# Opening both blocks of a two-block network on unscaled pairs, with the norms computed behind the first chunks

## The reference

```python
def first_block(x, ...):                      # DEPTH = 2
    cos, sin = rope_tables(positions, A_HEAD_DIM)
    for l in range(DEPTH):
        h = rms_norm(x, norm_mix[l])          # x * rsqrt(mean(x*x) + eps) * gain
        (m_qk, m_v, m_o, m_i, m_f, r_x, r_g, a_q, a_k, a_v, a_qi, a_ki, a_w, gates) = jnp.split(
            h @ w_in[l], split_at, axis=-1)
        ...  # y_a: mLSTM of m_*; y_b: gelu(r_g) * gated LRU of a causal conv of r_x;
        ...  # y_c: attention over the 64 keys that an indexer (a_qi, a_ki, a_w) selects; q, k, qi, ki get rope
        x = x + (g_a * (y_a @ w_b[0]) + g_b * (y_b @ w_b[1]) + g_c * (y_c @ w_b[2])) @ w_out[l]
        h = rms_norm(x, norm_ffn[l])
        ff_g, ff_u = jnp.split(h @ ffn_up[l], 2, axis=-1)
        x = x + (jax.nn.gelu(causal_dwconv(ff_g, ...)) * ff_u) @ ffn_down[l]
    return rms_norm(x, norm_final)
# second block: h = rmsnorm(x, gain) with 16 meta tokens ahead; h @ w_in gives z, x, B, C, dt, b, c, h;
# y1 = group_rmsnorm(ssd(x, B, C, dt) * silu(z)); y2 = group_rmsnorm(c * conv(b * h));
# x = x + [y1, y2] @ w_out; then a mixture of 16 experts (top 2) and a last norm.
```

## Time and profile before

| | |
|---|---|
| time, median of 3 runs | 1719.89 us (1718.14 to 1720.11) |
| time of the profiled execution | 1718.21 us |
| its span | 1716.3 us |
| PE busy | 1616.0 us (94%), 11632 matmuls |
| DVE busy | 1300.1 us (76%) |
| ACT busy | 951.9 us (55%) |
| POOL busy | 43.2 us (3%) |

### The profile page before, as it was taken

One profiled execution on the slowest core, in us unless ns is written; L12 is line 12 of the kernel. 1 busy time (PEld: TensorE's weight loads), 2 busy tenths in 40 slices (PEclk: granted clock), 3 DMA queues, 4 the chain that ended last, 5 costly groups with the idle time before them and its releaser, 6 DMA issues.

```text
span 1716.3 us, 28017 instructions
## 1 busy us (share of the span) xinstructions
PE 1616.0 (94%) x11632; PEld 1508.1 (88%) x11632; DVE 1300.1 (76%) x1567; ACT 951.9 (55%) x990; POOL 43.2 (3%) x43
## 2 busy tenths in 40 slices
PE   3998999999997988999999997799999999999998
PEld 3898999999997988999999997698899788888886
DVE  6699676676666699677676667885895788898886
ACT  5647454554444646555454444554553677777774
POOL 0100001000000010001000000000000000000000
PEclk9999999999998999999999999899999899999999
DMA  7444535555555444535555555254445499999993
GB/s 204 148 123 131 165 123 172 166 190 182 180 183 143 147 124 134 162 123 172 171 187 187 178 184 158 74 172 123 123 148 190 168 358 352 362 352 369 353 353 130
DMA packets 222399, 328.92 MB, mean 192 GB/s; under 512 B 20832, under 2 KB 179168, under 8 KB 222304
## 3 DMA queue, kind: packets, MB, share of 16 engines
q1 hardware_dynamic: 222304, 327.56, 57.8%
HBM read 326.49 MB, written 1.05 MB: 191 GB/s over the span
## 4 chain that ended last, share of the span: by engine, by line
PE 77%; DVE 15%; issue 3%; ACT 3%; DMA 1%; POOL 0%; SPq 0%; DVEq 0%; ACTq 0%
PE bank L2021 23%; PE bank L2022 23%; PE bank L2023 23%; DVE w_lo L1197 2%; ACT w_hi L697 1%; DVE work L1249 1%; DVE work L1354 1%; PE bank L2375 1%; DMA w_raw<-in_w_in 1%; DVE w_lo L1650 1%; PE bank L2481 1%; DVE work L1679 1%; DVE work L1302 1%; DVE work L1372 1%; PE bank L2534 1%
## 5 line engine op out<-in xcount | busy, mean ns | idle before, releaser
L1197 DVE TENSOR_TENSOR w_lo<-w_raw,w_hi 128x2048 fp32r<-128x2048 f32 x158 | 362.7, 2296 | 138.9 <-ACT w_hi L697 138.2
L2021 PE MATMUL bank<-act_h,w_hi 128*128 128x256 f32 (+1 forms) x1408 | 408.7, 290 | 27.9 <-DVE act_l L1233 9.5
L2023 PE MATMUL bank<-act_h,w_lo 128*128 128x256 f32 (+1 forms) x1408 | 399.8, 284 | 0.0
L2022 PE MATMUL bank<-act_l,w_hi 128*128 128x256 f32 (+1 forms) x1408 | 399.7, 284 | 0.0
L697 ACT CAST w_hi<-w_raw 128x2048 fp32r<-128x2048 f32 x158 | 300.5, 1902 | 43.0 <-PE bank L2023 34.3
L2021 PEld LDWEIGHTS bank<-act_h,w_hi 128*128 128x128 f32 x1408 | 269.6, 191 | 36.8 <-issue 31.8
L2022 PEld LDWEIGHTS bank<-act_l,w_hi 128*128 128x128 f32 x1408 | 269.8, 192 | 0.6
L2023 PEld LDWEIGHTS bank<-act_h,w_lo 128*128 128x128 f32 x1408 | 269.2, 191 | 0.0
L2022 PE MATMUL bank<-u_l,w_hi 128*128 128x256 f32 x768 | 217.3, 283 | 0.0
L2023 PE MATMUL bank<-u_h,w_lo 128*128 128x256 f32 x768 | 216.9, 282 | 0.0
L2021 PE MATMUL bank<-u_h,w_hi 128*128 128x256 f32 x768 | 215.9, 281 | 0.0
(11 more groups left out here) (446 smaller groups left out, 2911.8 us busy)
## 6 DMA issues: line engine op xcount, KB each, us to landing
w_raw<-in_w_in SPq DMA_DIRECT2D x88, 1024.0 KB, 5.5
w_raw<-in_ffn_up SPq DMA_DIRECT2D x48, 1024.0 KB, 5.2
w_raw<-in_e_gate SPq DMA_DIRECT2D x26, 1024.0 KB, 7.1
w_raw<-in_ffn_down SPq DMA_DIRECT2D x24, 1024.0 KB, 5.0
w_raw<-in_e_up SPq DMA_DIRECT2D x23, 1024.0 KB, 7.1
w_raw<-in_e_down SPq DMA_DIRECT2D x23, 1024.0 KB, 7.3
w_raw<-in_w_out SPq DMA_DIRECT2D x16, 1024.0 KB, 5.2
w_raw<-in_w_branch SPq DMA_DIRECT2D x12, 1024.0 KB, 5.1
```

The costliest lines, as they stand in the source:

```text
L1197: V.tensor_tensor(w_lo[c % RING][:], w_raw[c % RING][:], w_hi[c % RING][:].bitcast(F32), ALU.subtract).then_inc(sem[f"lo_ready{c % RING}"], 1)
L2021: mm(out, a_hi, b_hi, start=first, stop=False, skip_group_check=True)
L2022: mm(out, a_hi, b_lo, start=False, stop=False, skip_group_check=True)
L2023: return mm(out, a_lo, b_hi, start=False, stop=last, skip_group_check=True)
```

## The change

**First block.** All chunks c below `SCALED_FROM` (10) multiply the pair of x*gain. The pair is written while the residual sums of the layer before still come. The norm's sum runs on PE behind chunk 0, and `before` holds no scaled tiles any more. Chunks 0..3 (`RAW_OUT`) are read out of PSUM by DVE, multiplied by `u_r`, into `raw_out`, from where ACT and DVE go on as before; for 4..9 the rope tables are multiplied by `u_r` instead, and the small projections get a multiply of their own. From c=10 on the scaled pair is used as before; it is made in `side` of c=4..9. `small_lower` and `decay_base` move from ahead of chunk 0 to c=1 and c=2, ACT's sin and cos of the tables into c=1 of the first layer. The last FFN round is written out with `ffn_hidden` ahead of the split of the next layer's chunk 0 (it was behind it).

**Second block.** z0 and z1 come first and multiply the unscaled pair (`RAW_2`). Both norms come from one pass over the squares: PE sums them by token with and without the squared gain (`both_sums`), DVE and ACT work on columns of 128 x 2 (`both_norms`), PE turns them to rows (`rows_of_tokens`, between the halves of chunk 1). The meta tokens are normalised in the FFN before. The residual `hx` is written at c=2..5 (`stream_2`). Everything that hung on x, B, C and the SSD stands two chunks later; `SC_STEPS` is unchanged.

The numbers of the order:

```diff
+SCALED_FROM = 10
+RAW_OUT = 4
...
+RAW_2 = 2
+SECTION_2 = ([("z", i) for i in range(RAW_2)] + [("x", i) for i in range(4)] + [("B", i) for i in range(2)]
+             + [("C", i) for i in range(2)] + [("z", i) for i in range(RAW_2, 4)] + [("c", i) for i in range(4)] + [("h", i) for i in range(4)]
...
-SSD_STEPS = (14, 16, 18, 20)
+SSD_STEPS = (16, 18, 20, 22)
```

SP, ahead of the first layer (only the column of inverse frequencies is loaded first, the rest of the constants, 448 KB, last; `par` ahead of the second chunk):

```diff
+            sp.dma_start(cst[:, K_INV:K_INV + 1], consts[:, K_INV:K_INV + 1], allow_slow_non_contiguous=True)\
+                .then_inc(sem["freq_loaded"], 16)
             load(0, 0, source(0, 0))
             sp.dma_start(x_t[:], xT.rearrange("(k p) t -> p k t", p=P)).then_inc(sem["x_loaded"], 16)
+            sp.dma_start(par_all[:], par_1.rearrange("l p n -> p l n")).then_inc(sem["par_loaded"], 16)
             load(0, 1, source(0, 1))
-            sp.dma_start(par_all[:], par_1.rearrange("l p n -> p l n")).then_inc(sem["par_loaded"], 16)
+            sp.dma_start(cst[:, 0:K_INV], consts[:, 0:K_INV]).then_inc(sem["const_loaded"], 16)
```

ACT (`before`, `side`, the end of the FFN):

```diff
             def before(L):
-                norm(L)
                 split(L, 2)
-                need(act, "small_landed", L, 64)
-                nc.scalar.copy(small_h, small_raw).then_inc(sem["small_hi"], 1)
-                need(act, "lam_abs", L, 1)
-                A(lt[1], lt[0], ACT.Exp, scale=-1.0).then_inc(sem["lam_exp"], 1)
+                raw_deviation(L, 0)
 
...
+                if 5 <= c <= 8:
+                    i = c - 5
+                    need(act, "scaled", L, 2 * i + 2)
+                    nc.scalar.copy(act_h[:, 2 * i:2 * i + 2, :], norm_f[i % 2]).then_inc(sem["act_hi"], 1)
...
+                ffn_gate(L, N_FF - 1)
+                split(L, MIX + 2, N_FF - 1)
+                ffn_mid(L, N_FF - 1)
+                ffn_hidden(L, N_FF - 1)
+                split(L, MIX + 3, N_FF - 1)
+                split(L, MIX + 4, N_FF - 1)
+                if L < DEPTH - 1:
+                    for i in range(4):
+                        raw_upper(L + 1, 0, i)
+                        raw_square(i)
```

DVE, first block:

```diff
+            def of_tokens(count):
+                return u_r.unsqueeze(1).to_broadcast([P, count, T])
+
+            def scaled_pair(L, i):
+
+                if i >= 2:
+                    need(dve, "act_lo", L, i - 1)
+                for h in range(2):
+                    k = 2 * i + h
+                    STT(norm_f[i % 2][:, h, :], x_t[:, k, :], pm[L][:, M_NORM + k:M_NORM + k + 1], u_r,
+                        ALU.mult, ALU.mult).then_inc(sem["scaled"], 1)
+
+            def scaled_lower(L, i):
+                need(dve, "act_hi", L, i + 1)
+                V.tensor_tensor(act_l[:, 2 * i:2 * i + 2, :], norm_f[i % 2],
+                                act_h[:, 2 * i:2 * i + 2, :].bitcast(F32), ALU.subtract).then_inc(sem["act_lo"], 1)
...
                 g = GROUP0[c]
+                ps = main[g % 2][:].rearrange("p (b t) -> p b t", b=2)
+                if c < RAW_OUT:
+                    need(dve, "group_done", L, g + 1)
+                    V.tensor_tensor(raw_out[c % 2], ps, of_tokens(2), ALU.mult).then_inc(sem["raw_out"], 1)
+                    ps = raw_out[c % 2]
...
             def before(L):
-                norm(L)
+                add_squares(L, 0, u_sq)
                 split(L, 2)
+                need(dve, "std_ready", L, 1)
+                step(V.reciprocal(u_r, u_std))
+
+            def small_lower(L):
                 need(dve, "small_hi", L, 1)
                 V.tensor_tensor(small_l, small_raw, small_h.bitcast(F32), ALU.subtract).then_inc(sem["small_lo"], 1)
...
+                if c == 1:
+                    small_lower(L)
+                if c == 2:
+                    decay_base(L)
...
+                    own(V.tensor_tensor(sin_r, sin_t[:], u_r, ALU.mult))
+                    own.settle()
+                    V.tensor_tensor(cos_r, cos_t[:], u_r, ALU.mult).then_inc(sem["rope_tables"], 1)
+                    need(dve, "small_done", L, 1)
+                    V.tensor_tensor(small_s, psum[6][:, 0:T], u_r, ALU.mult).then_inc(sem["small_scaled"], 1)
...
+                if 6 <= c <= 9:
+                    scaled_lower(L, c - 6)
+                if 4 <= c <= 7:
+                    scaled_pair(L, c - 4)
...
+                ffn_conv(L, N_FF - 1)
+                split(L, MIX + 2, N_FF - 1)
+                ffn_product(L, N_FF - 1)
+                ffn_hidden(L, N_FF - 1)
+                split(L, MIX + 3, N_FF - 1)
+                split(L, MIX + 4, N_FF - 1)
...
+                    if i and L < DEPTH - 1:
+                        raw_lower(L + 1, 0, i - 1)
+                    elif i:
+                        raw_lower_2(i - 1)
+                if L < DEPTH - 1:
+                    raw_lower(L + 1, 0, 3)
+                else:
+                    raw_lower_2(3)
```

DVE, second block (`both_norms` follows the split of chunk 2, `scaled_2` the read-out of z0):

```diff
+            def both_norms():
+
+                dve.wait_ge(sem["stat_act"], STAT_STD)
+                step(V.reciprocal(r_1, std_1))
+                step(V.tensor_tensor(var_2, psum[6][:, 1:4:2], r_1, ALU.mult))
+                V.tensor_tensor(var_2, var_2, r_1, ALU.mult).then_inc(sem["stat_dve"], 1)
+                dve.wait_ge(sem["stat_act"], STAT_STD_2)
+                step(V.reciprocal(std_2, std_2))
+                V.tensor_tensor(r_12, r_1, std_2, ALU.mult).then_inc(sem["stat_dve"], 1)
+
+            def scaled_2(i):
+
+                for k in (2 * i, 2 * i + 1):
+                    STT(norm_f2[:, k, META:TM], x_t[:, k, :], gain_u[:, k:k + 1], rows_r[:, 1, :], ALU.mult, ALU.mult)\
+                        .then_inc(sem["scaled"], 1)
+
+            def scaled_lower_2(i):
+                need(dve, "act_hi", DEPTH, i + 1)
+                V.tensor_tensor(act2_l[:, 2 * i:2 * i + 2, :], norm_f2[:, 2 * i:2 * i + 2, :],
+                                act2_h[:, 2 * i:2 * i + 2, :].bitcast(F32), ALU.subtract).then_inc(sem["act_lo"], 1)
+
+            def stream_2(i):
+
+                for k in (2 * i, 2 * i + 1):
+                    STT(hx[:, k, META:TM], x_t[:, k, :], p2[:, Q_NFIN + k:Q_NFIN + k + 1], rows_r[:, 0, :],
+                        ALU.mult, ALU.mult).then_inc(sem["scaled"], 1)
+
...
+                if c < RAW_2:
+                    for half in range(2):
+                        g = 2 * c + half
+                        need(dve, "group_done", DEPTH, g + 1)
+                        V.tensor_tensor(zs[:, g, :], psum[g % 4][:, 0:T], rows_r[:, 1, :], ALU.mult)\
+                            .then_inc(sem["z_raw"], 1)
...
+                if 2 <= c <= 5:
+                    stream_2(c - 2)
```

PE (the bank wait, the operands of a chunk, the opening of a layer, the sums and the opening of the second block):

```diff
+                if c < RAW_OUT:
+                    need(pe, "raw_out", L, c + 1)
...
+                x_h, x_l = (u_h, u_l) if c < SCALED_FROM else (act_h, act_l)
+                if c == SCALED_FROM:
+                    need(pe, "act_lo", L, 4)
...
-                norm(L, 0)
                 for c in range(MIX):
                     chunk(L, c)
+                    if c == 0:
+                        norm(L, 0)
                     side(L, c)
...
+            def both_sums():
+
+                need(pe, "squares", DEPTH, 4)
+                for k in range(KT):
+                    for s in range(2):
+                        ins = mm(psum[6][:, 2 * s:2 * s + 2], norm_f2[:, k, META + s * P:META + s * P + P],
+                                 gain_2[:, k, :], start=k == 0 and s == 0, stop=k == KT - 1, skip_group_check=True)
+                ins.then_inc(sem["stat_pe"], 1)
+
+            def rows_of_tokens():
+
+                pe.wait_ge(sem["stat_dve"], STAT_R)
+                for n, r in enumerate((r_1, r_12)):
+                    for s in range(2):
+                        ins = mm(psum[7][:, n * T + s * P:n * T + s * P + P], r[:, s:s + 1].to_broadcast([P, P]), ident,
+                                 start=n == 0 and s == 0, stop=True, skip_group_check=True)
+                ins.then_inc(sem["stat_pe"], 1)
...
+            chunk_2(0)
+            both_sums()
+            chunk_2(1, rows_of_tokens)
+            for c in range(2, MIX_2 - 1):
```

More of the change, by code:

```diff
@@ L945, in layer @@
                 own_each = 1
[L946 removed]
+                with act.Fori(1, N_FF - 1) as n:
                     own.enter(n - 1, own_each)
@@ L964, in _ @@
             act.wait_ge(sem["par_loaded"], 16)
+            for i in range(4):
+                raw_upper(0, 0, i)
+            split(0, 1)
+            for i in range(4):
+                raw_square(i)
             for L in range(DEPTH):
@@ L2078, in chunk @@
                 ins.then_inc(sem["group_done"], 1)
-            rows_first = [(m, k) for m in range(2) for k in range(KT)]
-            pairs_first = [(m, 2 * i + j) for i in range(4) for m in range(2) for j in range(2)]
             def norm(L, which):
                 need(pe, "squares_added", L, which + 1)
-                mm(psum[7][:, 0:T], ones[:, 0:P], (u_sq if which else norm_f)[:, 0, :], start=True, stop=True)\
+                mm(psum[7][:, 0:T], ones[:, 0:P], u_sq[:, 0, :], start=True, stop=True)\
```

484 lines of the change are left out of this document (268 added, 216 removed).

## The result

The changed kernel takes 1741.81 us (median of 4 runs, 1738.81 to 1742.80) against 1720.00 (4 runs) of the one before: 1.0126 times as long, 95% interval 1.0114 to 1.0138. It is 22 us slower; the forecast was 2.5 us slower (1722.4), with a range of 1709 to 1729.

What follows compares the result with a forecast made beforehand. PE was taken as 94% busy, but DVE as full from the LRU step on, so earlier PE starts count only if DVE's stretches start earlier. First layer -2.0, second +3.2, second block +1.3: +2.5, forecast 1722.4 us, range 1709 to 1729.

Steps and rivals of the forecast that it cites:

- the fourth multiply: Layer 2: DVE's queue, 28 us behind 550.2, ends the fourth multiply by 1/rms at 578.2.
- the way from there to L1559: Layer 2: ACT's queue from the fourth multiply to L1478 (now L1559) takes 15.2 us, so 593.4 against 596.11.
- the price of what stands behind L1478: Each layer, up to the conv before chunk 16: four scaled pairs (3.3) and four subtracts (2.7) cost DVE 5.9 us.
- the chance of slower (0.34): Whole kernel: slower by over 0.2%, summed from A 0.19 (the forecast itself), D 0.12 and G 0.03.
- The wait ahead of chunk 24: Second block: PE waits 4.6 us for the fourth lower part of y1, at the end of DVE's cycle of c=23.
- PE restarted: Second block's opening: PE starts at 1065.9, behind the last residual sum and the pair; x0 follows at 1084.1.
- +1.3: Second block's net term, a loss in us: 5.8 gained up to C B, nothing left of it after chunk 24.
- D: Rival, slower, 0.12: twelve new operations a layer cost more than their rows beside POOL; +5.6 us, 1728.
- G: Rival, slower by ACT, 0.03: ACT stands 1.4 us behind each of two table loads before L1478; +5.5 us, 1728.
- B: Rival, faster by PE's pace, 0.15: fourth multiply comes with PE, L1478 is 9.4 and 14.4 earlier; -10.7 us, 1709.
- C: Rival, faster by the second block alone, 0.13: last y1 pair not late, 4.6 to 7 us gone; 1715 to 1718.

Runs made afterwards that it cites:

- both moves: Changed kernel with the scaled pairs three chunks earlier and the second block's last y1 pair one step earlier: 1714.17 us, 0.9964 of the kernel before.
- the sums spread: Against scaled pairs three chunks earlier plus last y1 pair one step earlier: 16 column sums set among z0's last eight products; 1712.62 us, 0.9950 of before.
- two chunks earlier: Scaled pairs two chunks earlier than in the changed kernel, not three, with the last y1 pair early and column sums among z0's products: 1712.64 us, 0.9959.
- the subtracts on POOL: Against scaled pairs three chunks earlier plus last y1 pair one step earlier: DVE's four subtracts a layer moved to POOL; 1717.31 us, 0.9984 of before.

## Why the prediction was wrong

**What bounds the kernel.** Right: DVE sets the pace from the LRU step on, and an earlier PE is worth only what reaches it. L1559 is 8.9 and 2.8 earlier where 7.9 and 2.7 were forecast; PE's restart (550.29 less the shift of 7.0 is 543.3) came as worked out, and so did, to half a microsecond, the fourth multiply (its end at 584.65 is 577.7 less the shift, for 578.2) and the way from there to L1559 (15.7 for 15.2).

**The step that failed** is the price of what stands behind L1478: "the change puts four scaled pairs ... and four subtracts ... there", 5.9 us, "I count no cover". I priced the operations and not the order that came with them. The diff shows `if c == SCALED_FROM: need(pe, "act_lo", L, 4)`, a wait added on PE, and I didn't ask what is queued behind it and who waits for that. From the trace of before it could be worked out: DVE's last operation of chunk 9 ends at 118.5, PE begins chunk 10 at 108.2, so the wait is over 10 us; and DVE's next w_lo wants the buffer of chunk 10, so DVE stands while PE does that chunk and ACT its w_hi. The row of 77.45 us busy in 80.1 says that DVE has no idle time, not that nothing can give it some. The term measures 4.4 for the operations and 11.1 for DVE's idle time, in each layer; 2 x 11.1 put on the forecast's 1722.4 make 1744.6, and less 2 x 1.5 for the smaller price of the operations 1741.6. That this is within 0.2 of the measured time is partly luck: the misses that follow cancel. They are small and of both signs (1.0 us of the first layer's start to the good, 1.6 of the second block to the bad). No rival had this circle in it, so the chance of slower (0.34) rested on other causes.

**Second block.** The wait ahead of chunk 24 was right (4.7 for 4.6, and 4.4 us came back when it was taken away). PE restarted at 1086.34 less the 20.4 of shift, 1065.9, as forecast, but x0 began at 1086.0 and not at 1084.1: I took z0 and z1 at 2.4 GHz. Behind the 2.1 us of idle z0 ran five matmuls 0.12 us apart and then 16 at 1.2 GHz, and z1 behind the small ones ran 17 at 1.2 GHz. The traces price this. From the restart to x0 it is 20.1 us in the changed kernel with two such stretches and 18.63 with one (both moves); with the sums spread it is 18.94 with one and 17.48 with none (two chunks earlier): 1.5 each. So the clock's part, some 3 us, is more than the 1.9 by which x0 is late, and the rest of that way was shorter than worked out. That this makes up the difference between +1.3 and the +2.9 measured is likely and not shown: DVE is full behind x0, and no run took the two stretches away from the changed kernel alone.

**The rivals.** D and G did not happen. L1288 and L1293 took their rows' time (0.48 and 0.69; POOL met none of them), and ACT's activation followed the table load at once, at 598.14 behind 596.85 + 1.28. That POOL can double them is true, as the run with the subtracts on POOL shows. (D's own sum has a slip: at twice the price 5.9 becomes 11.8 a layer; the 8.7 that it used is the price when half of the operations double.) B did not happen either: L1559 came 8.9 and 2.8 earlier, where B wanted 14.4 and 9.4. C's mechanism was real when made: the last y1 pair can be early, and it is worth 4.4.

**What stays open.** The best kernel here gains 7.2 us over the one before, although PE starts 14.2, 8.6 and 17.0 us earlier at the changed kernel's three openings (the last two less the shifts). PE's wait for DVE's copy of the rope (L1380 in the changed kernel, 17.4 us over both layers, 14.4 in the kernel with the sums spread) says that the early start still ends at DVE, some 9 us behind L1559. Whether less work for DVE there would let it through was not tried.

## What to carry to other kernels

Ask of each added wait not only how long the waiting engine stands, but whether the engine it waits for needs, a few operations later, something that the waiting one releases (a buffer, a bank). Where the slower engine sets the pace, the other's lead is a cushion: a wait that uses it up costs nothing until the slower one runs out of input. From then on it costs what lies between the release and the slower engine's next input, here PE's chunk and two operations of ACT, and not the length of the wait that one sees in the list. Moving such a wait by one chunk was worth 23 us here. New work on the full engine cost no more than its rows say (4.4 us of 5.8 a layer); what was dear was to make it idle.

## What the runs showed of the hardware

- A stop of PE of 2.1 us ahead of z0 was followed by 1.2 GHz within z0 in five of the ten traces that have it (the changed kernel after five matmuls at full speed; the one with the sums spread at once, 0.61 granted) and not in the other five (both moves among them). Where it came in these two it lasted some 16 matmuls, 1.5 us lost. Behind the wait of 12.6 us 27 matmuls ran at 1.2 GHz, 2.6 us lost.
- The row of 32 matmuls with two columns, 3.5 us in which PE shows as busy, had the low clock in its last part or right behind it in all eight traces that have the row (0.53 and 0.57 granted at z1's start in the changed kernel and with both moves), and in neither of the two in which the small ones stand among large ones.
- POOL and DVE side by side can slow each other: 0.88 to 1.89 us and 1.23 to 2.21 on DVE, 1.27 to 2.60 on POOL for the same operation, while DVE's w_lo kept its 2.28.
